# Eight buffers and an earlier start for the gathered expert rows, sixteen words ahead, and a bank-by-bank start of the second expert layer

## What is computed

```python
# h: (520, 1024); u_tab, v_tab: (16384, 1024); 8 heads, 16 choices each
eidx, gate = top16 product-key search (q @ sub_keys)
a    = gelu(h . u_tab[eidx])          # (520, 128)
f    = sum over e of gate * a * v_tab[eidx]
x    = x + gate2 * RMSNorm_post2(f)
```

## Time and profile before

| | us |
|---|---|
| median of 3 timed runs | 1737.69 |
| the three runs | 1737.2, 1737.69, 1745.22 |
| the profiled execution | 1741.56 |
| its span, first to last instruction | 1739.8 |
| PE busy | 1707.9 |
| DVE busy | 1051.0 |
| POOL busy | 1055.3 |
| ACT busy | 557.9 |

### The profile page before, as it was taken

The page is one execution under the profiler, slowest core; times in us unless marked ns, Lnnn a source line. Parts: engine busy times, 40 slices in busy tenths (PEclk is TensorE's granted clock), DMA queues, the critical chain, the costliest instruction groups (busy, mean ns, idle before and its releaser), DMA issues.

```text
span 1739.8 us, 31278 instructions
## 1 busy us (share of the span) xinstructions
PE 1707.9 (98%) x12766; PEld 1674.1 (96%) x12766; DVE 1051.0 (60%) x2186; ACT 557.9 (32%) x754; POOL 1055.3 (61%) x709
## 2 busy tenths in 40 slices
PE   8999999999999999999999999999999999999996
PEld 6999879799999999999999999999999999999996
DVE  5624473765776457676632222126888789888885
ACT  4122244432333323233322222223333333333332
POOL 0430100228868888888888878855677787666621
PEclk9999999999999999999999999999999999999998
DMA  9999352623666665757586666678999899999971
GB/s 369 384 294 322 116 201 99 237 90 39 130 145 138 124 142 112 151 121 150 111 170 139 141 137 139 140 200 318 384 371 353 333 370 363 365 370 365 381 293 50
DMA packets 191415, 385.20 MB, mean 221 GB/s; under 512 B 73352, under 2 KB 131144, under 8 KB 176424
## 3 DMA queue, kind: packets, MB, share of 16 engines
q1 hardware_dynamic: 110760, 306.47, 51.9%
q0 software_dynamic: 80512, 76.74, 20.4%
HBM read 318.44 MB, written 64.19 MB: 220 GB/s over the span
## 4 chain that ended last, share of the span: by engine, by line
PE 77%; POOL 2%; DMA 1%; DVE 1%; issue 1%; ACT 0%; DVEq 0%; ACTq 0%
PE ps L1726 42%; PE ps L1749 27%; PE ps L625 5%; DMA qp<-vtab,packed_choice 1%; PE ps L1700 1%; POOL qp L1885 1%; POOL ag L1878 1%; DVE qp L2037 0%; DVE h L2060 0%; PE ps L1710 0%; DVE fg L1970 0%; PE ps L871 0%; DVE x L2067 0%; DVE ul L1920 0%; PE ps L1775 0%
## 5 line engine op out<-in xcount | busy, mean ns | idle before, releaser
L101 POOL DMA_INDIRECT gates_dram<-gate,where x384 | 644.6, 1679 | 191.3 <-issue 177.7
L1726 PE MATMUL ps<-hh,ul 128*128 128x260 f32 x2048 | 412.8, 283 | 0.0
L1726 PE MATMUL ps<-hl,uh 128*128 128x260 f32 x2048 | 412.8, 283 | 0.0
L1726 PE MATMUL ps<-hh,uh 128*128 128x260 f32 x2048 | 412.1, 283 | 0.0
L1920 DVE TENSOR_TENSOR ul<-us,uh 128x1024 fp32r<-128x1024 f32 x132 | 161.2, 1222 | 350.6 <-ACT uh L1784 343.6
L1749 PE MATMUL ps<-cl,uh 128*128 128x384 f32 (+1 forms) x1024 | 345.6, 337 | 5.1 <-DVE ul L1920 3.6
L1749 PE MATMUL ps<-ch,uh 128*128 128x384 f32 x1024 | 344.8, 337 | 0.0
L1749 PE MATMUL ps<-ch,ul 128*128 128x384 f32 x1024 | 344.6, 337 | 0.0
L1726 PEld LDWEIGHTS ps<-hl,uh 128*128 128x128 f32 x2048 | 315.7, 189 | 0.4 <-issue 0.4
L1726 PEld LDWEIGHTS ps<-hh,ul 128*128 128x128 f32 x2048 | 315.7, 188 | 0.0
L1726 PEld LDWEIGHTS ps<-hh,uh 128*128 128x128 f32 x2048 | 314.8, 188 | 0.0
(11 more groups left out here) (250 smaller groups left out, 2058.5 us busy)
## 6 DMA issues: line engine op xcount, KB each, us to landing
us<-utab SPq DMA_DIRECT2D x128, 512.0 KB, 4.0
pairs<-vtab SPq DMA_DIRECT2D x62, 1024.0 KB, 8.6
gates_dram<-blank SPq DMA_DIRECT2D x24, 1024.0 KB, 12.4
ahead_dram<-a SPq DMA_DIRECT2D x128, 192.0 KB
qp<-ahead_dram SPq DMA_DIRECT2D x32, 768.0 KB, 6.9
gt<-gates_dram SPq DMA_DIRECT2D x32, 768.0 KB, 9.1
wr<-w_ada SPq DMA_DIRECT2D x20, 1024.0 KB, 6.1
wr<-w_in SPq DMA_DIRECT2D x14, 1024.0 KB, 9.7
```

What stands on the lines that cost most here:

```text
L101: nc.gpsimd.indirect_dma_start(out=io["gates"].rearrange("g p c a t -> (g p c a t)").unsqueeze(1), out_offset=bass.IndirectOffsetOnAxis(ap ...
L1726: last = nc.tensor.matmul(out[:, half, :], w, r[:, k, half * TH:(half + 1) * TH], start=(k == 0 and q == 0), stop=(k == KD - 1 and q == 2))
```

## The change

Six things, each small:

1. Eight row buffers instead of four (`NG`), the other four on the tile `h`. That tile held the scores of the search, which is over by then.
2. POOL requests the first eight rows right behind its last scatter, before it waits for the stores of `a[126]` and `a[127]`.
3. Behind that wait it requests sixteen words (`WORDS_AHEAD`) instead of eight, then goes on with word `r + 16` and row `r + 8`. The row waits for sum `r`.
4. The first sums stand at block 6 instead of 8 (`G0`); the end of their schedule stays at block 123.
5. PE waits, in block 0 only, bank pair by bank pair: none of the gelus for banks 0 and 1, gelu 126 for banks 2 and 3, gelu 127 for banks 4 and 5, gelu 125 for banks 6 and 7.
6. The semaphores of the four loads of `x` are shared with the pairs' (`rows_in`), which makes four free for the new buffers. The counts that are waited for rise by 16.

```diff
--- before.py
+++ after.py
@@ -296,6 +296,7 @@
         on_h = h[:].rearrange("p k t -> p (k t)")
         io["s"] = on_h[0:TT, 0:2 * PH * NK].rearrange("p (j n) -> p j n", n=NK)
         io["s2"] = on_h[0:TT, 2 * PH * NK:4 * PH * NK].rearrange("p (j n) -> p j n", n=NK)
+        io["rows_in"] = [sem(f"rows_in{n}") for n in range(KD // 2)]
         io["w_in_ok"] = [sem(f"w_in{n}") for n in range(NW)]
         io |= {n: sem(n) for n in ("in_keys", "s_mm", "s_ok", "settled", "best_ok", "ex_ok", "pick_ok", "qp_ok", "wl_ok")}
         on_chip = (x, h, mod, cst, gain, co, tsm, rs, ps)
@@ -392,7 +393,7 @@
             return n - NSLOT - EXTRA if n < 2 * NSLOT + EXTRA else n - NSLOT
 
         w_slot = [sem(f"w_slot{n}") for n in range(NSLOT + EXTRA)]
-        in_x = [sem(f"in_x{n}") for n in range(KD // 2)]
+        in_x = io["rows_in"]
         first_ts, first_hs, first_hk, first_hh, first_hl = (
             sem(n) for n in ("first_ts", "first_hs", "first_hk", "first_hh", "first_hl"))
         in_c, in_cst, in_trig, in_state, in_misc = (
@@ -1475,7 +1476,7 @@
 def peer_stage(nc, sem, sb, pair, halves, on_chip, hh, hl, packed, qp, io):
     x, h, mod, cst, gain, co, tsm, rs, ps = on_chip
     ones, ident, iota = cst[:, 0, :], cst[:, 1, :], cst[:, 2, :]
-    NH, NA, NV, NL, NG = 3, 2, 2, 3, 4
+    NH, NA, NV, NL, NG = 3, 2, 2, 3, 8
     LEAD = 2
     TD = SEQ // 4
     NP, FIRST_PAIR = 4, 2
@@ -1484,7 +1485,8 @@
     EVERY = 9
     LAST = 2 * NK
     GCH = 8
-    G0 = 8
+    WORDS_AHEAD = 2 * GCH
+    G0 = 6
     GROUP_AT = [sum(n for _, n in GROUPS[:g]) for g in range(len(GROUPS) + 1)]
     PACK_AT, PACKED_AT = 84, 88
     FOLDS = (64, 32, 16, 8)
@@ -1516,8 +1518,10 @@
         ul = sb(stack, "ul", [P, NH, KD * P], F32R)
         a = sb(stack, "a", [P, NA, T])
         on_q = qp[:].rearrange("p j t -> p (j t)")
-        vg = on_q[:, 0:NG * D].rearrange("p (n d) -> p n d", n=NG)
-        aa = on_q[:, NG * D:NG * D + NV * GB * ND].rearrange("p (n a t) -> p n a t", n=NV, a=GB)
+        on_h = h[:].rearrange("p k t -> p (k t)")
+        vg = [where_to[:, n * D:(n + 1) * D] for where_to in (on_q, on_h) for n in range(NG // 2)]
+        aa_at = NG // 2 * D
+        aa = on_q[:, aa_at:aa_at + NV * GB * ND].rearrange("p (n a t) -> p n a t", n=NV, a=GB)
         packed.close()
         pairs = sb(stack, "pairs", [P, NP, 2, D], F32, "right")
 
@@ -1531,7 +1535,7 @@
             j = (m - NK) // 2
             if j < FIRST_PAIR:
                 return w_in[m % NW], 16 * (m // NW + 1)
-            return v_in[j % NP], 16 * ((j - FIRST_PAIR) // NP + 1)
+            return v_in[j % NP], 16 * ((j - FIRST_PAIR) // NP + 2)
 
         gt = sb(stack, "gt", [P, NV, NCH, GB, CH])
         ch = sb(stack, "ch", [P, NL, ND], F32R)
@@ -1550,7 +1554,7 @@
 
         w_in, s_mm, s_ok, settled, best_ok, ex_ok, pick_ok = (
             io[n] for n in ("w_in_ok", "s_mm", "s_ok", "settled", "best_ok", "ex_ok", "pick_ok"))
-        v_in = [sem(f"v_in{n}") for n in range(NP)]
+        v_in = io["rows_in"]
         uh_ok = sem("uh_ok")
         ul_ok = sem("ul_ok")
         w_mm = sem("w_mm")
@@ -1736,12 +1740,13 @@
                         scores(i, 2, 4)
 
             pe.wait_ge(s_ok, 4 * TILES)
-            pe.wait_ge(a_ok, NK)
             for n in range(NK):
                 m = NK + n
                 pe.wait_ge(ul_ok, m + 1)
                 pe.wait_ge(cl_ok, n + 1)
                 for k in range(KD):
+                    if n == 0 and k in (2, 4, 6):
+                        pe.wait_ge(a_ok, NK - (NK - k // 2) % 3)
                     hi, lo = (w[:, m % NH, k * P:(k + 1) * P] for w in (uh, ul))
                     for q, (w, r) in enumerate(((hi, cl), (hi, ch), (lo, ch))):
                         whole = n == 0 and q == 0
@@ -1870,22 +1875,33 @@
                     scatter(nc, io, i, r)
 
             pool.wait_ge(packed_in, 16)
+
+            def gather_word(r):
+
+                nc.gpsimd.indirect_dma_start(
+                    out=ag[:, r:r + 1], out_offset=None, in_=words,
+                    in_offset=bass.IndirectOffsetOnAxis(ap=packed_choice[:, 0, r:r + 1].bitcast(U32), axis=0))\
+                    .then_inc(ag_in[r // GCH % 4], 16)
+
+            def gather_row(r):
+
+                nc.gpsimd.indirect_dma_start(
+                    out=vg[r % NG], out_offset=None, in_=values,
+                    in_offset=bass.IndirectOffsetOnAxis(ap=packed_choice[:, 1, r:r + 1].bitcast(U32), axis=0))\
+                    .then_inc(vg_in[r % NG], 16)
+
+            for r in range(NG):
+                gather_row(r)
             for m in range(NK - NA, NK):
                 pool.wait_ge(*stored(m))
-            for r in range(-GCH, TG):
-                if r + GCH < TG:
-                    at = r + GCH
-                    nc.gpsimd.indirect_dma_start(
-                        out=ag[:, at:at + 1], out_offset=None, in_=words,
-                        in_offset=bass.IndirectOffsetOnAxis(ap=packed_choice[:, 0, at:at + 1].bitcast(U32), axis=0))\
-                        .then_inc(ag_in[at // GCH % 4], 16)
-                if r >= 0:
-                    if r >= NG:
-                        pool.wait_ge(fg_ok, r - NG + 1)
-                    nc.gpsimd.indirect_dma_start(
-                        out=vg[:, r % NG, :], out_offset=None, in_=values,
-                        in_offset=bass.IndirectOffsetOnAxis(ap=packed_choice[:, 1, r:r + 1].bitcast(U32), axis=0))\
-                        .then_inc(vg_in[r % NG], 16)
+            for r in range(WORDS_AHEAD):
+                gather_word(r)
+            for r in range(TG):
+                if r + WORDS_AHEAD < TG:
+                    gather_word(r + WORDS_AHEAD)
+                if r + NG < TG:
+                    pool.wait_ge(fg_ok, r + 1)
+                    gather_row(r + NG)
 
             for n, k in enumerate(ON_POOL):
                 pool.wait_ge(t_ok, k + 1)
@@ -1967,7 +1983,7 @@
                 if r:
                     dve.wait_ge(fg_ok, r)
                 sums_of = fg[:, group_of(r), :]
-                nc.vector.scalar_tensor_tensor(sums_of, vg[:, r % NG, :], ag[:, r:r + 1], sums_of,
+                nc.vector.scalar_tensor_tensor(sums_of, vg[r % NG], ag[:, r:r + 1], sums_of,
                                                ALU.mult, ALU.add).then_inc(fg_ok, 1)
 
             def fold(n):
```

## The result

The changed kernel takes 1753.4 us (median of 6 runs, 1746.89 to 1757.18), the kernel before 1739.96 us (median of 6, 1737.2 to 1745.22): a ratio of 1.0073, with an interval of 1.0049 to 1.0096. It is slower, where 1744.0 us were forecast, and it lies above the forecast's range of 1732 to 1749 us. The profiled execution took 1746.89 us, the fastest of the six, with a span of 1745.1 us.

The account below looks back on a forecast made before the run. PE, busy for 98% of the span, was taken as the bound. Rows +8.3, clock +1.5 and steady state -5.1 gave +4.7 us; 1744 us was the middle between 1742.4 (stall in the median) and 1746.3 (1.2 us of it), range 1732 to 1749.

Parts of the forecast that it names:

- Eight rows earlier: Change of layers: early rows delay the store of a[125] and gelu 127 by 9.4 us, block 1 by +8.3 us.
- block 1 waits for the low part anyway: Change of layers: block 1 starts only after its low part, so bank by bank gives nothing back in the changed kernel.
- The clock: Change of layers: PE idles for two spells, the clock falls once more, +1.5 us, between 0 and 3.
- The eight buffers' steady state: Second layer: eight buffers remove the stall at 1362 us, where DVE waited for gathered rows and PE for a low part: -5.1 us.
- bound from the other side: Steady state of the second layer: if the stall comes partly from POOL's issue, not buffer depth, it stays: 0.
- rival C: Second layer: POOL too late to fill the deeper buffers, the stall at 1362 us stays; about 1747 us, chance 0.06.
- Bank by bank: Block 0: an earlier start alone gives -1.2 us, limited by block 1's low part; nothing back in the changed kernel.
- Sums from block 6: Second layer: one sum per 3.6 us instead of 3.55, costing 0.
- Sixteen words: Near block 6: first eight words land at 1209 us, DVE may wait 1 us but has it to spare: 0.
- A: Change of layers: the rows hide and gelu 127 keeps its time; 1731.4 or 1735.3 us, chance 0.25.
- A2: Change of layers: half of the delay, as the store overtakes some rows; about 1739 us, chance 0.13.
- B: Blocks 4 and 5: the pairs of v_tab come late and PE waits; 1748.5 us, chance 0.11.

Follow-up runs that it names:

- e3: The kernel before with only PE's bank-by-bank wait in block 0 added: 1736.42 us, ratio 0.9995.
- e6: The kernel before with eight row buffers instead of four and the shared semaphores, requests in the old order, one wait for all gelus: 1737.8 us, ratio 0.9993.
- e7: The kernel before with eight row buffers, shared semaphores and the bank-by-bank wait, rows not requested early: 1736.13 us, ratio 0.9976.
- e5: The kernel before with its four row buffers filled right behind the last scatter, nothing else changed: 1744.64 us, ratio 1.0044.
- e2: The changed kernel run again, unchanged, for a second trace: 1745.87 us, ratio 1.0044 to the kernel before.
- e13: The changed kernel run a fourth time, unchanged, as yardstick for its group: 1745.95 us, ratio 1.0055 to the kernel before.
- e17: The changed kernel run a fifth time, unchanged, beside eight buffers with bank by bank: 1749.74 us, ratio 1.0072 to the kernel before.
- e11: The changed kernel run a third time, unchanged: 1753.12 us, ratio 1.0069 to the kernel before.
- e1: The changed kernel with its first eight row requests moved behind the wait for the stores of a[126] and a[127]: 1750.16 us, ratio 1.0067.
- e4: The changed kernel with POOL waiting for the store of a[125] before its first eight rows: 1746.54 us, ratio 1.0039.
- e8: The changed kernel with three buffers for a instead of two, the words' tile moved onto the keys, one semaphore shared: 1749.18 us, ratio 1.0054.
- e12: The kernel before with an unused tile of 32 bytes behind the buffers of a, nothing else changed: 1751.53 us, ratio 1.0067.
- e15: The changed kernel with the first sums at block 8 as before, instead of block 6: 1747.16 us, ratio 1.0058.
- e16: The changed kernel with words requested eight ahead instead of sixteen: 1828.24 us, ratio 1.0518.

## Why the prediction was right and wrong

In this table, all times are starts in one trace of each kernel, in us behind E, the end of the first layer's last matmul. (Before, the last matmul of layer two starts at 1720.1 us; 1716.8 us is where the chain of waits leaves PE.) The median is that of the timed runs; before, it is that of the five later groups.

| | gelu 127 | block 1 | last matmul | median |
|---|---|---|---|---|
| before, its one profile | 0.79 | 6.19 | 543.36 | 1737.3 to 1738.1 |
| e3, bank by bank alone | 0.98 | 5.26 | 537.09 | 1736.42 |
| e6, eight buffers alone | 0.84 | 6.24 | 537.96 | 1737.8 |
| e7, with bank by bank | 0.78 | 5.06 | 536.88 | 1736.13 |
| e5, four rows early | 5.61 | 13.25 | 544.97 | 1744.64 |
| changed, e2 | 10.01 | 15.10 | 547.40 | 1745.87 |
| changed, e13 | 10.92 | 15.56 | 547.28 | 1745.95 |
| changed, e17 | 10.34 | 14.99 | 552.13 | 1749.74 |
| changed, first trace | 10.35 | 15.09 | 549.98 | 1753.4 |
| changed, e11 | 9.87 | 14.96 | 557.57 | 1753.12 |

**Eight rows earlier: right, in mechanism and nearly in size.** The forecast had gelu 127 9.4 us later; it is 9.1 to 10.1 us later. It had gelu 126 some 5 us later and block 0 near 1178.6 us, that is E + 1.9; gelu 126 is 5.7 to 8.3 us later and block 0 starts between E + 1.7 and E + 4.3. It had +8.3 us at block 1; the traces show +8.8 to +9.4 (15.0 to 15.6 less 6.2). The dose (e5) and the cuts (e1 and e4 by the place of the rows, e8 by the buffer) show that it goes from the rows through DMA to the store of `a[125]` and the buffer. The queues shared one for one before that store, as the earlier trace rows had them: 597 packets of each from 1166 to 1176 us. The Trainium skill's round-robin between queues ("DMA: Bandwidth & Descriptors", Queues, rings and completion order) fits these traces. Its 358 GB/s per core (the same page, Bandwidth), which the prediction set against the measurement, is the page's figure for two cores that stream from one memory at once; for one core alone the page has 425 GB/s measured, and the windows here, up to 422 GB/s from one core, agree with that.

One link was wrong: "block 1 waits for the low part anyway", with PE idle ahead of it. The low part did come 4.2 us behind gelu 127, as forecast (E + 14.57 us), but block 0's second half at half clock ended 0.5 us later still (0.4 to 0.9 us in the five traces), and PE was not idle ahead of block 1.

**The clock: +1.5 us forecast, 0.4 to 1.5 us found.** Part of it is these 0.4 to 0.9 us, which already stand in block 1's place. The rest comes behind block 1: from there to the last matmul e2 takes 532.3 us, e13 531.7 and e6 531.7. Counted from E to the last matmul, both terms together were forecast at 9.8 us; e2 and e13 are 9.4 and 9.3 us above e6.

**The eight buffers' steady state: the step that failed.** The prediction put this term at -5.1 us, "bound from the other side" at 0, and took half of the stall off its forecast. But for rival C, with a chance of 0.06, it had no case in which the steady state behind the change of layers costs anything. Measured, the term is 0 at best, and in three of the changed kernel's five groups +4 to +7 us stand in its place.

First, the gain. The stall at 1362 us was sized rightly in the trace where it was seen (to the last matmul, 543.4 us before against 538.0 in e6), but it isn't in the median. The prediction saw that the median of before, 3.9 us under the profiled execution, "looks like a run with little of the 5.1 us stall", and then gave half of it away all the same. The traces e3, e5 and e12, with four buffers too, don't have it. The later groups have medians of 1737.3 to 1738.1 us, with most runs from 1735 to 1738.5 and a third or fewer above 1740.4. Taking the stall out (e6) measured 0.9993 (0.9978 to 1.0009). With that term at zero the same sum is 1737.5 + 8.9 + 0.6 = 1747.0 us. The two groups without the new stalls measured 1745.87 and 1745.95. This alone would have left the result inside the range.

Second, the cost. What carried the result over the upper end of 1749 us are the new stalls: 1749.74, 1753.4 and 1753.12 us in three groups, against 1745.9. In e17 and e11 the traces show them. For the first result they are an inference: its only trace is of the fastest run, 1746.89 us, and shows 2.6 us of them (549.98 against 547.40 us to the last matmul), and its group's kernel before was slower too, 1739.96 us. They came with eight buffers only, but whether the buffers make them isn't shown, and why some groups have them and others not is open.

**The other parts.** Bank by bank: forecast as nothing in the changed kernel, and -1.2 us alone; alone it moves block 1 by 0.9 us and the median by an amount that can't be told from zero (e3). Inside the changed kernel "gives nothing back" was too strict. Without it block 0 would start behind gelu 127, near E + 10.7 us, and if it took the 6.93 us of e5, block 1 would come near E + 17.6 us instead of 15.1: an estimate of 2.5 us, which wasn't run by itself. Sums from block 6: 0, right (e15). Sixteen words: forecast 0 beside the old eight, right in the sum, but read wrongly (e16). In none of the five traces of the changed kernel did DVE wait for the words at block 6.

**The rivals.** A and A2 (the rows hide, in all or in half) fell with gelu 127 at E + 10. B (pairs late) did not happen: PE has no wait around blocks 4 and 5 in any trace of the changed kernel. C (DVE still waits for rows) did not either: that row has no counterpart after. No rival had the new stalls.

**A better version.** Eight buffers with bank by bank, without the early rows, was 0.9976, 0.9993 and 1.0037 in three groups. The first is a gain that its interval bears out, the last a loss, and each group had another chip. So nothing here beats the kernel before reliably. Bank by bank alone costs nothing in any trace and gains too little to be measured.
